# The opening of a fused transformer block: x and ctx loaded first, and conditioning columns computed in blocks that finish two k tiles of h

## The reference, cut to what matters

```python
mod   = silu(c)     @ w_mod + b_mod                 # (1, 6*2048)
sh1, sc1, g1, sh2, sc2, g2 = split(mod, 6)
mod_c = silu(c_ctx) @ w_mod[:, :4096] + b_mod[:4096]
shc, scc = split(mod_c, 2)

h  = rms_norm(x,   norm_mix_pre) * (1 + sc1) + sh1  # (256, 2048)
hc = rms_norm(ctx, norm_mix_pre) * (1 + scc) + shc  # (256, 2048)
y  = hybrid_mixer(h, hc, w_in, ...)                 # p = h @ w_in, pc = hc @ w_in[:, :3616]
x1 = x + g1 * rms_norm(y, norm_mix_post)
h  = rms_norm(x1, norm_ffn_pre) * (1 + sc2) + sh2
out = x1 + g2 * rms_norm((silu(h @ w_gate) * (h @ w_up)) @ w_down, norm_ffn_post)
```

## Time and profile before

| | us |
|---|---|
| median of 3 runs | 1740.43 |
| lowest and highest of them | 1739.21, 1740.7 |
| span of the profiled execution | 1739.5 |
| PE busy in it | 1712.4 (98%) |
| DVE, ACT, POOL busy | 996.1 (57%), 742.6 (43%), 160.2 (9%) |
| moved by DMA | 420.09 MB, mean 241 GB/s |

### The profile page before, as it was taken

How to read it: one execution, slowest core, us unless ns; L and a number is a source line. 1 busy time by engine, 2 the same in 40 slices (tenths; PEclk the granted TensorE clock), 3 DMA queues, 4 the chain that set the end, 5 groups by cost and what they waited for, 6 DMA issues and landing times.

```text
span 1739.5 us, 21419 instructions
## 1 busy us (share of the span) xinstructions
PE 1712.4 (98%) x7889; PEld 1384.6 (80%) x7889; DVE 996.1 (57%) x1097; ACT 742.6 (43%) x833; POOL 160.2 (9%) x176
## 2 busy tenths in 40 slices
PE   6999999999999999999999999999999999999998
PEld 2458888888878888888888888888888888888886
DVE  2446767748766686676665654544544544444444
ACT  3334222226655454455444564444444444443442
POOL 0010000000045354230000000000000000000000
PEclk8999999999999999999999999999999999999999
DMA  9999999968888575656777666666666666766662
GB/s 366 368 382 386 355 338 362 368 255 308 314 310 281 172 227 178 205 172 205 236 226 248 185 196 191 190 186 191 188 187 191 188 187 190 262 193 194 193 193 93
DMA packets 183835, 420.09 MB, mean 241 GB/s; under 512 B 12896, under 2 KB 13248, under 8 KB 173920
## 3 DMA queue, kind: packets, MB, share of 16 engines
q1 hardware_dynamic: 167680, 375.45, 65.6%
q0 software_dynamic: 7344, 28.46, 4.9%
q10 hardware_dynamic: 8752, 15.38, 2.3%
HBM read 398.74 MB, written 20.50 MB: 241 GB/s over the span
## 4 chain that ended last, share of the span: by engine, by line
PE 95%; DVE 2%; DMA 1%; issue 1%; ACT 1%; SPq 0%; DVEq 0%; POOLq 0%; POOL 0%; ACTq 0%
PE ps L1524 27%; PE ps L1528 27%; PE ps L1536 27%; PE ps L1606 2%; PE ps L1580 2%; DMA raw<-in_w_mod 1%; PE ps L1622 1%; PE ps L1810 1%; PE ps L1826 1%; PE ps L1864 1%; PE ps L1781 1%; PE ps L1687 0%; PE ps L1569 0%; PE ps L1920 0%; DVE xr_t L410 0%
## 5 line engine op out<-in xcount | busy, mean ns | idle before, releaser
L1021 DVE TENSOR_TENSOR w_lo<-raw,w_hi 128x1024 fp32r<-128x1024 f32 x492 | 608.4, 1239 | 539.9 <-ACT w_hi L634 539.8
L634 ACT ACTIVATE w_hi<-raw 128x1024 fp32r<-128x1024 f32 x488 | 515.9, 1060 | 793.7 <-PE ps L1536 780.5
L1524 PE MATMUL ps<-w_hi,h_hi 128*128 128x512 f32 x1456 | 457.9, 395 | 1.1 <-DVE h_lo L1423 1.1
L1528 PE MATMUL ps<-w_hi,h_lo 128*128 128x512 f32 x1456 | 450.2, 389 | 0.0
L1536 PE MATMUL ps<-w_lo,h_hi 128*128 128x512 f32 x1456 | 396.6, 389 | 0.0
L1528 PEld LDWEIGHTS ps<-w_hi,h_lo 128*128 128x128 f32 x1456 | 273.3, 188 | 57.5
L1536 PEld LDWEIGHTS ps<-w_lo,h_hi 128*128 128x128 f32 x1456 | 273.3, 188 | 57.1
L1524 PEld LDWEIGHTS ps<-w_hi,h_hi 128*128 128x128 f32 x1456 | 269.9, 188 | 56.5 <-issue 1.8
L1033 DVE SCALAR_TENSOR_TENSOR acc<-wm,csil,acc 128x2048 f32<-128x2048 f32 x60 | 141.0, 2350 | 54.7 <-DMA wm<-in_w_mod 54.7
L1524 PE MATMUL ps<-w_hi,hid_hi 128*128 128x512 f32 x352 | 109.8, 389 | 0.0
L1528 PE MATMUL ps<-w_hi,hid_lo 128*128 128x512 f32 x352 | 109.6, 389 | 0.0
(11 more groups left out here) (303 smaller groups left out, 1395.0 us busy)
## 6 DMA issues: line engine op xcount, KB each, us to landing
raw<-in_w_in SPq DMA_DIRECT2D x184, 512.0 KB, 6.4
wm<-in_w_mod SPq DMA_DIRECT2D x64, 1024.0 KB, 7.0
raw<-in_ffn_w_gate SPq DMA_DIRECT2D x88, 512.0 KB, 4.4
raw<-in_ffn_w_up SPq DMA_DIRECT2D x88, 512.0 KB, 4.4
raw<-in_ffn_w_down SPq DMA_DIRECT2D x88, 512.0 KB, 4.8
raw<-in_w_mod SPq DMA_DIRECT2D x64, 512.0 KB, 7.9
raw<-in_w_out SPq DMA_DIRECT2D x32, 512.0 KB, 4.7
px<-stage ACTq DMA_DIRECT2D x44, 256.0 KB, 5.9
```

Source lines behind the costliest of these rows:

```text
L634: act.activation(w_hi[:, j % SPLIT, :, :], raw[:, j % RAW, :, :], ACT.Copy).then_inc(w_high, 1)
L1021: dve.tensor_tensor(w_lo[:, j % SPLIT, :, :], raw[:, j % RAW, :, :], w_hi[:, j % SPLIT, :, :].bitcast(F32), ALU.subtract).then_inc(w_low, 1)
L1524: pe.matmul(o, hi[:, kk, c], w_hi[:, q, e, :], start=kk == 0, stop=False)
L1528: pe.matmul(o, lo[:, kk, c], w_hi[:, q, e, :], start=False, stop=False)
```

## The change

1. **Loads.** x and ctx are loaded before the first place. A w_mod slot now holds 256 shift columns and 256 scale columns, and is loaded by two DMAs, one for each half of its columns; a w_in slot of the opening is loaded by two DMAs too, one for each k tile. `landed_at` counts the two.
2. **Blocks.** Block n gives shift and scale of k tiles 2n and 2n+1, so each block completes one pair of k tiles of h, where two blocks completed two pairs.
3. **Places.** Pair i of w_in is loaded with block i+1 (its ctx slot ahead of it, its lat slot after three w_mod slots), and the last pair within block 7, so that the last place is a w_mod slot. Before, five W slots stood behind the last w_mod slot.
4. **PE's order.** x is transposed first (three tiles of it before the first w_mod slot). In block n PE does the last third of ctx pair n-2, the transposes of block n-1, w_mod slot 0, lat pair n-2, slots 1 and 2, a third of ctx pair n-1, slots 3 and 4, a third of it, and slots 5, 6, 7. Of a ctx pair the high-high products come first, the products with `w_lo` second, and those with `h_lo` last, for every pair (before: for pairs 6 and 7 alone).
5. **ACT and DVE** follow the new order. `mod_t` is laid out by blocks; `modulate` runs once for each block, with two additions of the bias in place of one.

```diff
+HALF = N // 2
...
-        opening = []
-        for n in range(MOD_BLOCKS):
+        opening = [("mod", 0, j) for j in range(8)]
+        for n in range(1, MOD_BLOCKS):
+            opening.append(("ctx", n - 1))
             for j in range(8):
                 opening.append(("mod", n, j))
-                if j == 2 and n >= CTX_LAG:
-                    opening.append(("ctx", n - CTX_LAG))
-                if j == 0 and n > CTX_LAG:
-                    opening.append(("lat", n - CTX_LAG - 1))
-        opening += [("lat", 5), ("ctx", 6), ("lat", 6), ("ctx", 7), ("lat", 7)]
+                if j == 2:
+                    opening.append(("lat", n - 1))
+                if j == 4 and n == MOD_BLOCKS - 1:
+                    opening += [("ctx", n), ("lat", n)]
...
+                for h in range(2):
+                    if what[0] == "mod":
+                        n, k = what[1], 2 * what[2]
+                        sp.dma_start(raw[:, q, :, h * HALF:(h + 1) * HALF],
+                                     w_mod_k[:, k:k + 2, h * D + n * HALF:h * D + (n + 1) * HALF])\
+                          .then_inc(landed[q], 16)
+                    else:
+                        col = 0 if what[0] == "ctx" else N
+                        sp.dma_start(raw[:, q, h, :], w_in_k[:, 2 * what[1] + h, col:col + N]).then_inc(landed[q], 16)
...
-            take_mod_row(0)
             square_x(0)
             square_x(1)
+            take_x(0)
             square_x(2)
-            take_x(0)
+            take_x(1)
             square_x(3)
-            for m in range(1, 4):
-                take_x(m)
+            take_x(2)
+            take_x(3)
+            take_mod_row(0)
             for n in range(1, MOD_BLOCKS):
-                if n >= CTX_LAG:
-                    split_open("ctx", n - CTX_LAG)
+                split_open("ctx", n - 1)
+                high_pair(2 * n - 2)
+                split_open("lat", n - 1)
+                if n == MOD_BLOCKS - 1:
+                    split_open("ctx", n)
+                    split_open("lat", n)
                 take_mod_row(n)
...
+            for n in range(MOD_BLOCKS):
+                modulate(n)
+                scale_pair(dve, 2 * n, "h1_ready")
+                if n < MOD_BLOCKS - 1:
+                    split_open("ctx", n)
+                low_pair(dve, 2 * n, "h1_lo")
+                if n < MOD_BLOCKS - 1:
+                    split_open("lat", n)
+                if n == MOD_BLOCKS - 2:
+                    split_open("ctx", n + 1)
+                    split_open("lat", n + 1)
...
+            turn_rows()
+            for m in range(3):
+                turn_x(m)
             for n in range(MOD_BLOCKS):
+                if n >= 2:
+                    ctx_part(n - 2, 2)
                 if n >= 1:
-                    pe.wait_ge(S("mod_row_ready"), n)
+                    take_mod_columns(n - 1)
                 for j in range(8):
                     mod_slot(n, j)
-                    if n == 0 and j == 3:
-                        turn_rows()
...
+                    if n == 0 and j == 1:
+                        turn_x(3)
...
+                    if n >= 2 and j == 0:
+                        lat_part(n - 2)
+                    if n >= 1 and j == 2:
+                        ctx_part(n - 1, 0)
+                    if 1 <= n < MOD_BLOCKS - 1 and j == 4:
+                        ctx_part(n - 1, 1)
+            ctx_part(MOD_BLOCKS - 2, 1)
             take_mod_columns(MOD_BLOCKS - 1)
-            ctx_part(5, 2)
-            lat_part(5)
-            for i in range(6, 8):
-                for r in range(3):
+            for i in range(MOD_BLOCKS - 2, MOD_BLOCKS):
+                for r in range(2 if i == MOD_BLOCKS - 2 else 0, 3):
                     ctx_part(i, r)
                 lat_part(i)
```

More of the change, by code:

```diff
@@ L703, in split_open @@
                 place, o = place_of[kind, i], open_number((kind, i))
-                act.wait_ge(landed[place % RAW], 16 * (place // RAW + 1))
+                act.wait_ge(landed[place % RAW], landed_at(place))
                 if o >= SPLIT:
@@ L949, in split_next @@
                 q = (S_FFN + j) % RAW
[L950 removed]
+                act.wait_ge(landed[q], landed_at(S_FFN + j))
                 act.wait_ge(w_used, S_FFN - 2 * SPLIT + j + 1)
@@ L1575, in mod_slot @@
                 place = place_of["mod", n, j]
-                pe.wait_ge(landed[place % RAW], 16 * (place // RAW + 1))
+                pe.wait_ge(landed[place % RAW], landed_at(place))
                 for e in range(2):
@@ L1585, in ctx_part @@
             def ctx_part(i, r):
[L1587 removed]
+                o = open_number(("ctx", i))
                 q = o % SPLIT
[L1589 to L1596 removed]
+                steps = (((0, h_hi, hc_hi, w_hi), (1, h_hi, hc_hi, w_hi)),
+                         ((0, h_hi, hc_hi, w_lo), (1, h_hi, hc_hi, w_lo)),
+                         ((0, h_lo, hc_lo, w_hi), (1, h_lo, hc_lo, w_hi)))[r]
                 if r == 0:
[L1598 removed]
+                    pe.wait_ge(S("h1_hi"), i + 1)
                     pe.wait_ge(w_high, o + 1)
[L1600 removed]
+                if r == 1:
                     pe.wait_ge(w_low, o + 1)
[L1602 removed]
+                if r == 2:
                     pe.wait_ge(S("h1_lo"), i + 1)
```

122 lines of the change are left out of this document (37 added, 85 removed).

## The result

The changed kernel takes 1753.74 us (median of 4 runs, 1752.54 to 1754.33) against 1740.51 for the kernel before (1739.21 to 1740.7): a ratio of 1.0075, 95% interval 1.0061 to 1.009. That is 13.2 us more, where 4.9 were forecast: the sign was right, the size was not, and the time lies above the range of 1737.5 to 1751.5.

The account below looks back on a forecast made before the run. PE, 98% busy, bounds the kernel, with DMA level in the opening. Last w_mod slot at 136.2 us plus 15.1 of work ends the opening at 151.3 against 146.4: +4.9, 1745.3 us, range 1737.5 to 1751.5.

Parts of the forecast that it names:

- The tail behind the last slot: PE work behind the opening's last w_mod slot: 15.14 us in place of 24.62, a gain of 9.5, without waiting for h.
- The price of a row: Opening's DMA: a 1 KB row takes 47.5 ns, so a w_mod slot takes 1.52 us in place of 1.36.
- rival 1: Opening's loads: halved rows cost nothing, 42.5 ns each, PE sets the block; -3.3 us, 1737.1 us; chance 0.14.
- The hole at the start: Gap in the load stream, as load 8 waits for PE behind three x tiles: 1.3 us, bounds 0 and 5.5.
- rival 2: Slow start: PE at its low clock, the stream stands still 5.5 us, not 1.3; +9.1 us, 1749.5 us; chance 0.14.
- the sum up to the opening's end: Last w_mod slot done at 136.2 us, plus 15.1 of PE work: opening ends at 151.3 against 146.4, +4.9 us.
- Behind the opening: nothing: Stage after the opening: DMA has 17 us of lead where it had 22, share 0.91, PE waits for none: no cost.
- Unpaired slots: PE's block in the opening grows from 13.45 to 14.5 us, hidden behind the DMA's block of 15.0: no cost.
- The way from span to median: Whole kernel: the median of the runs lies 0.9 us above the profiled execution, 1745.3 for 1744.4 us.
- Rivals 3 and 4: Opening: 3, it evens out within 3 us, 1741 us, chance 0.18; 4, h isn't ready, ctx work doesn't move, chance 0.02.

Follow-up runs that it names:

- e8: The changed kernel with ACT squaring x tiles 0 and 1 ahead of its `cols` copy, and PE taking w_mod slots 0 to 3 one x tile sooner: 1750.29 us.
- e12: The changed kernel with the edits of e8 and e9, and the last ctx and lat W slots loaded behind the last w_mod slot: 1748.22 us.
- e9: The changed kernel with the conditioning rows kept in another tile, so the first column chunks don't wait for block 7's columns: 1751.56 us.
- e2: The kernel before with every opening slot loaded by two DMAs, one for each k tile, rows still 2 KB: 1743.44 us, ratio 1.0014.
- e15: The changed kernel with GpSimd's loads of the constants held back until the context stream is 28 products in: 1750.33 us.
- e16: The changed kernel with finished products put behind an even number of slots, so all conditioning slots run in pairs: 1755.28 us.
- e18: e12 with GpSimd's loads of the constants held back as in e15: 1743.07 us, ratio 1.0014.
- e19: e18 with 2 KB rows, so shift and scale come from other columns than the reference's: 1738.34 us, ratio 0.9983.

## Why the prediction was wrong in size

- **The tail behind the last slot: right.** 15.14 us forecast, 155.64 - 140.48 = 15.16 measured. The gain of 9.5 us is real, and h is ready in time.
- **The price of a row: right.** 47.5 ns forecast, 47.0 measured; the block 15.0 and 14.7. The rule of the Trainium skill, DMA: Bandwidth & Descriptors, section Specifications, that was weighed against it (line rate from 512 B on) does not hold here: rows of 8 KB, of 2 KB and mostly of 1 KB move 426, 387 and 357 GB/s. So rival 1 falls.
- **The hole at the start: the first step that failed.** 1.3 us were put for it, and it costs 4 to 6 (6.05 by the opening's end in e8's profile, 4.2 by the ratios). Three parts of the chain were missed. ACT's copy of `cols` stands ahead of the first square and waits for small rows that land at 9.2 us: the transposes begin at 14.11, and in e8 at 11.24, where the forecast's own chain gives 6.8 + 4.25 = 11.05. I had taken ACT free when x lands, though that copy is in its program. Second, slots 0 and 1 are done at 27.4, not 23.7, partly at the low clock. Third, the stream does not come back at once: 275 GB/s over 28 to 38 us, where e8 has 354. The low clock in the second is rival 2's mechanism, and rival 2 priced the hole at 5.5 us, for an opening's end of 151.3 + 4.2 = 155.5; it was 155.64. But the low clock was the smaller part: the third tile's transposes took 2.38 us and the 8 matmuls 1.94, where 1.97 and 1.06 are their times at the full clock, 1.3 us together; the late `cols` moved the chain by 2.9 (14.11 against e8's 11.24). That rival 2 came so near with a part of the cause is luck. The forecast without its 1.3 is 150.0, and e8, without a hole, has 149.59 in its fastest execution: the rest of the sum up to the opening's end comes out within a microsecond or two.
- **That sum held partly by luck.** The W slots within block 7 make PE wait 3.0 us, and the last two slots then take 3.41 us at a low clock in place of 2.1 for two slots alone; without these e12 ends 2.6 us sooner than e8 (e9's edit, which e12 has too, gave 0.6 by itself). The sum had the bytes of these two slots but no wait and no clock for them. The block's 0.3 us under forecast, seven times, may pay for much of that; it was not measured apart. Two DMAs a slot, which I put at 0.7 us of completion writes, cost 2.4 us in before's order (e2); in the new order the stream stays full in mid-opening, and no run measures the term.
- **"Behind the opening: nothing": the second step that failed.** It costs 3.5 us. The prediction let SP wait for the columns until 138.6 and held the stream full; SP waited until 143.1, and the stream fell to 246 GB/s behind it. I had seen that the constants' loads come 14 us later (they come 19 later, 143.4 against 124.6) and asked only when they are first used, not what they pass on the way: they fall into the 17 us in which the column chunks must land. Taking away either, the wait (e9) or the constants (e15), brings the stretch back. The DMA share of 0.91 over 274 us is a mean and says nothing of these 17.
- **Unpaired slots: right**, hidden with 1 KB rows (e16), and PE's block was 14.35 for 14.5 forecast.
- **The way from span to median**: 1.3 us in the profiled pair and not 0.9. With 4.3 us of the opening's end and 3.5 of the stretch, 0.4 here and rounding, that is the whole miss of 8.4 us.
- **Rivals 3 and 4 fall**: nothing evened out, and the change does what it says.

The terms also add up the other way, by the spans of the profiled executions: after 1752.4; without the hole 1746.8 (e8); with free chunks and the W slots behind the last w_mod slot 1745.3 (e12); with the constants later 1741.0 (e18); with 2 KB rows 1734.8 (e19); before has 1739.5. So the new order, with long rows and the other edits, gains 4.7 us on before by the spans and 3.0 by the ratio, and the halved rows take away more than that (6.2 by the spans, 5.4 by the ratio). These steps were made in this order; another order could divide them otherwise, and each span is of one execution.

## What to carry to other kernels

When a change delays the point that several queues wait for, list every load which that point releases, on all queues, and look at the window of ten or twenty microseconds in which they now meet: a mean DMA share over the stage hides it. When a load moves to the front, follow the first consumer's engine program from its first instruction, with every small copy that stands ahead. An order that gains a tail but halves the rows of a stream at its limit must be charged for both, and an earlier end is worth only what the next stage's loads can follow.

## What the runs showed of the hardware

- With GpSimd's queue at work beside SP's, 1.15 MB of the first take 43.7% of the engines' time and 2.18 MB of the second 57.3%: the small loads take almost half of the time, and more for each MB (38% against 26%).
- Twice as many DMAs for the same bytes and rows cost 0.14% of the kernel (e2). From 49 to 140 us the rate fell from 376 to 358 GB/s, in stretches behind SP's waits; between them it did not fall. That the time to issue is the cause is argued, not tested.
- With the 4 MB of x and ctx under way, 16 KB of small rows (`rows` from b_mod) took 5.93 us from issue to landing in the changed kernel (3.18 to 9.11), and ACT's whole x chain stood behind them.
- In the changed kernel a wait of 3.0 us up to 135.6, in a stage where PE was else busy, was followed, one slot later, by 8 matmuls that took 3.41 us in place of 2.1 for two slots alone, mostly at the low level of 1.2 GHz (mean granted clock 0.72 over 135 to 141). e8 has the same: a wait of 2.97 us, then 12 matmuls in 4.05 us, clock 0.72 over 129 to 135. In e12, with waits of 0.45 us, PE kept 2.4 GHz (1.00 over 131 to 141).
